# Powers of GpSimd later in its order, conv state stored in rows, the sample's indices copied earlier: a streaming encoder step on one core

## The chip, the core and the metric

The kernel runs on one core of a Trainium2 chip, as one program. The metric is the device time of one execution in microseconds. Three timed executions of the kernel before took 3982.19, 3983.57 and 3987.05 us; the median, 3983.57 us, is the time before.

## The reference, cut to what matters

One layer of a streaming encoder is computed for 1024 prompt rows and 32 sample rows. All arrays are fp32.

```
xn = rmsnorm(x);  z = xn @ w_in          # conv B | conv C | conv h | q | k | v | 2 gates
u  = C * h;  conv = B * dwconv3_causal(u)            # new state: last 2 rows of u
q, k = rope(rmsnorm(q)), rope(rmsnorm(k))            # 8 heads, two components each
o  = (softmax(Q1 K1^T) - lam * softmax(Q2 K2^T)) V;  o = rmsnorm(o) * (1 - lam0)
x  = x + (sig(gA) * (conv @ w_conv_out) + sig(gB) * (o @ w_attn_out)) @ w_o
# PEER, for each row and each of 8 heads:
q  = rmsnorm(xn2 @ wq);  s = q . subkeys             # 2 x 128 scores
best 16 of the 16 x 16 sums -> 16 experts e, weights g = softmax(best)
x  = x + sum_k g_k * gelu(u[e_k] . xn2) * v[e_k]     # 128 experts for each row
```

A row of 1024 values of `u` and one of `v` lie side by side in memory, 8 KB for each expert. The outputs are y, k and v of prompt and sample, and the two last rows of u of each (`conv_prompt` and `conv_sample`, 2 x 1024 each).

## The kernel before

**Rows and passes.** The rows are nine tiles: eight of 128 prompt rows (t = 0 to 7) and one of the 32 sample rows (t = 8). They go in three passes, rb = 0, 1 and 2, over tiles 0 to 2, 3 to 5, and 6 to 8. Each pass has two halves. `attend` goes through eight heads and three tiles: project, normalise and rotate q and k, scores, softmax, difference, weigh values, normalise the output. `middle` multiplies with the weight blocks `wall`: conv (24 blocks, in passes 1 and 2), gates and branch outputs (32), w_o (8), wq (16), and then searches the best keys (`find_tops`). Each block is 512 KB, loaded by SyncE into six buffers `low` (`load_mid`, L473), one when the block six places ahead of it has been used.

**The gather stream.** PEER has 1056 slots: 128 for each prompt tile, and 32 for the sample, whose 32 rows are spread four times over the 128 partitions. For slot q GpSimd gathers 128 rows of 8 KB, 1 MB, into buffer q % 8 of a ring (`gather`, L701), once slot q - 8 has been used. VectorE takes the dot product (`dot`, L1610), ScalarE makes gelu, weight and a diagonal (`slot`, L1224 to L1235), and TensorE adds weight times v (`weigh`, L991), in some slots VectorE (`add_row`, L1621). TensorE is one slot behind.

**What sets the order.** Every engine's program is written out from one list of positions. A position is a slot number; slots before 0 (from START = -340) have no gather. Each engine runs its generators up to position q and then does its part of slot q. GpSimd's own place is ahead of the others, since gather q waits only for slot q - 8: an instruction of GpSimd at position p + 8 comes about when the other engines are at p. GpSimd also makes the powers (x + eps)^-0.5: of q and k (`rr`, L672 and L674, after VectorE's `mean_square`, used by `scale_heads`), of the attention's output (`ro`, L663 and L666, after ScalarE's `square_out`, used by `norm_out`), of the row norm (`rx`) and of the PEER queries (`rq`, L689, four for each pass, after `find_tops` 3, 7, 11 and 15). POOL_LAG = 6 puts them 6 positions behind the step that makes their input; it stands in GpSimd's queue of gathers, and while a power waits for its input, no gather behind it is issued.

**Indices of the sample.** `routing` on VectorE chooses experts in 20 units; the last, of tile 8, ends at position 1017. The indices of tile 8 go into `idx[:, 0]`. At slot 1024 VectorE copies them and their weights into `idx[:, 1]` and `gw[:, 1]`, for each group of 32 partitions its own 32 slots (L1638, L1639), and raises `idx_ready`, on which gather 1024 waits.

**Conv state.** The last columns of u are kept as `ends_out`, channels in partitions. At m = 8 of the last pass SyncE stores them by four DMAs, one element in each run (L611), ahead of the weight loads that follow in its queue.

## Time and profile before

| | |
|---|---|
| median of three executions | 3983.57 us (3982.19 to 3987.05) |
| profiled execution, span from first to last instruction | 3979.7 us |
| its own time beside the span | not listed; the median is 3.9 us above the span |
| TensorE busy | 3171.9 us (80%) |
| VectorE busy | 2654.8 us (67%) |
| ScalarE, GpSimd busy | 1461.1 us (37%), 1531.1 us (38%) |
| moved by DMA | 1340.72 MB, of them 1108.54 MB by the gathers |
| mean granted TensorE clock | 0.872 |

The profile is of one execution. Busy shares are means over stages with different limits, so the stages have to be read one by one: the stretch up to about 600 us has no gathers; the attention of passes 1 and 2 lies at about 770 to 1250 us and 1800 to 2440 us; from about 3150 us on nearly only slots are left. DMA share is the busy share of the core's 16 DMA engines, GB/s what they moved in the stretch.

### The profile page before, as it was taken

What the parts mean: (1) busy time and instruction counts of PE and PEld (TensorE: products, weight loads), DVE (VectorE), ACT (ScalarE), POOL (GpSimd) and SP (SyncE); (2) the same over time, 40 slices, a digit from 0 to 9 for tenths busy, and PEclk for the clock granted to TensorE, in tenths of its full rate; (3) what the DMA queues carried; (4) which work ended last, traced back from release to release, by engine and by line L of the source; (5) the groups of instructions that cost most, each with busy time, mean ns of one, the idle gap of its engine ahead of it and who ended that gap; (6) DMA issues with size and microseconds to landing.
All of it is one profiled execution on the core that took longest, in us unless ns stands there. A gap on an engine that the chain in (4) does not pass through costs nothing.

```text
span 3979.7 us, 46667 instructions
## 1 busy us (share of the span) xinstructions
PE 3171.9 (80%) x14264; PEld 1436.6 (36%) x14264; DVE 2654.8 (67%) x6242; ACT 1461.1 (37%) x4359; POOL 1531.1 (38%) x1405
## 2 busy tenths in 40 slices
PE   6999988788987999797788887876879666666655
PEld 3555545333433554353333333544425211111110
DVE  3443016988888964778677876885568864556664
ACT  2222001355654244223456564233323333333332
POOL 2111002355655433434445554442344443444333
PEclk9999999889998999898899988888889776776676
DMA  4223336799999999988789999999999999999998
GB/s 157 97 92 102 101 122 257 266 354 340 408 365 387 416 417 392 403 342 342 293 333 375 377 352 397 416 362 368 400 420 404 370 420 420 420 420 419 411 394 346
DMA packets 257065, 1340.72 MB, mean 337 GB/s; under 512 B 31472, under 2 KB 70128, under 8 KB 121392
## 3 DMA queue, kind: packets, MB, share of 16 engines
q0 software_dynamic: 152400, 1108.54, 69.3%
q1 hardware_dynamic: 79344, 204.15, 14.0%
q10 hardware_dynamic: 25072, 25.04, 1.8%
q8 instruction: 115, 1.88, 0.2%
q14 instruction: 134, 1.10, 0.1%
HBM read 1310.49 MB, written 27.15 MB: 336 GB/s over the span
## 4 chain that ended last, share of the span: by engine, by line
PE 42%; DMA 24%; DVE 17%; ACT 6%; issue 4%; DVEq 3%; SPq 2%; ACTq 1%; POOL 1%; POOLq 0%
DMA ringx<-in_peer_uv,tl_idx 12%; DMA mix<-in_peer_uv,tl_idx 11%; PE tl_ps L939 9%; PE tl_ps L991 8%; PE tl_ps L775 6%; PE tl_ps L974 4%; PE tl_ps L923 3%; PE tl_ps L950 3%; PE tl_ps L840 3%; DVE ringx L1610 3%; DVE mix L1610 3%; PE tl_ps L753 2%; DVE tl_xa L1621 2%; PE tl_ps L809 2%; SPq L611 1%
## 5 line engine op out<-in xcount | busy, mean ns | idle before, releaser
L701 POOL DMA_INDIRECT mix<-in_peer_uv,tl_idx x528 | 626.0, 1186 | 782.9 <-PE tl_ps L991 432.8
L701 POOL DMA_INDIRECT ringx<-in_peer_uv,tl_idx x528 | 612.7, 1160 | 731.7 <-PE tl_ps L991 450.8
L1610 DVE CUSTOM_DVE_ANT_0 mix<-mix,tl_xb 128x1024 f32<-128x1024 f32 x528 | 640.9, 1222 | 296.2 <-DMA mix<-in_peer_uv,tl_idx 288.3
L1610 DVE CUSTOM_DVE_ANT_0 ringx<-ringx,tl_xb 128x1024 f32<-128x1024 f32 x528 | 640.7, 1222 | 277.8 <-DMA ringx<-in_peer_uv,tl_idx 270.1
L991 PE MATMUL tl_ps<-ringx,tl_dg 64*64 64x512 f32 x3352 | 569.7, 764 | 298.8 <-ACT tl_dg L1235 298.3
L991 PE MATMUL tl_ps<-mix,tl_dg 64*64 64x512 f32 x3288 | 566.9, 775 | 280.3 <-ACT tl_dg L1235 256.7
L1224 ACT ACTIVATE tl_hg<-tl_hd 128x1 f32<-128x1 f32 x1056 | 213.3, 202 | 1560.9 <-DVE tl_hd L1610 1545.8
L939 PE MATMUL tl_ps<-tl_xr,low 128*128 128x384 f32 (+1 forms) x1280 | 401.9, 470 | 32.2 <-DMA low<-in_wall 27.7
L1228 ACT ACTIVATE tl_hw<-tl_hg,tl_gw 128x1 f32<-128x1 f32 x1056 | 310.9, 294 | 76.1 <-issue 4.6
L991 PEld LDWEIGHTS tl_ps<-ringx,tl_dg 64*64 64x64 f32 x3352 | 105.6, 155 | 639.4 <-ACT tl_dg L1235 566.8
L991 PEld LDWEIGHTS tl_ps<-mix,tl_dg 64*64 64x64 f32 x3288 | 104.9, 157 | 617.8 <-ACT tl_dg L1235 512.6
L939 PEld LDWEIGHTS tl_ps<-tl_xr,low 128*128 128x128 f32 x1280 | 247.3, 197 | 201.0 <-issue 72.7
L1235 ACT ACTIVATE tl_dg<-tl_eye,tl_hw 128x64 f32<-128x64 f32 x830 | 288.6, 348 | 59.3 <-issue 1.7
L775 PE MATMUL tl_ps<-low,tl_xr 128*128 128x384 f32 (+1 forms) x768 | 298.5, 536 | 7.2 <-ACT tl_u L1101 7.0
L974 PE MATMUL tl_ps<-tl_xr,low 128*128 128x384 f32 (+1 forms) x768 | 262.6, 481 | 1.6 <-ACTq L1196 1.6
L923 PE MATMUL tl_ps<-tl_xr,low 128*128 128x384 f32 (+1 forms) x768 | 239.3, 471 | 0.6 <-ACT tl_xr L1080 0.6
L775 PEld LDWEIGHTS tl_ps<-low,tl_xr 128*128 128x128 f32 (+1 forms) x768 | 137.5, 189 | 185.0 <-issue 105.0
L974 PEld LDWEIGHTS tl_ps<-tl_xr,low 128*128 128x128 f32 x768 | 140.1, 195 | 135.2 <-issue 74.4
L923 PEld LDWEIGHTS tl_ps<-tl_xr,low 128*128 128x128 f32 x768 | 151.4, 201 | 102.5 <-issue 34.4
L672 POOL TENSOR_SCALAR tl_rr<-tl_ss 128x4 f32<-128x4 f32 (+1 forms) x72 | 61.5, 855 | 316.5 <-DVE tl_ss L1438 316.5
L1575 DVE TENSOR_TENSOR tl_u<-tl_ps,tl_u 128x384 f32<-128x384 f32 (+1 forms) x48 | 25.0, 521 | 197.5 <-PE tl_ps L939 195.3
L1621 DVE SCALAR_TENSOR_TENSOR tl_xa<-mix,tl_hw,tl_xa 128x1024 f32<-128x1024 f32 x117 | 149.8, 1281 | 3.7 <-issue 3.3
(193 smaller groups left out, 4002.1 us busy)
## 6 DMA issues: line engine op xcount, KB each, us to landing
low<-in_wall SPq DMA_DIRECT2D x240, 512.0 KB, 7.9
low<-in_watt SPq DMA_DIRECT2D x60, 512.0 KB, 9.0
mix<-in_peer_uv,tl_idx POOLq DMA_INDIRECT x528, 13.6
ringx<-in_peer_uv,tl_idx POOLq DMA_INDIRECT x528, 13.6
ringx<-in_watt SPq DMA_DIRECT2D x12, 512.0 KB, 5.9
tl_u<-in_x_prompt SPq DMA_DIRECT2D x8, 512.0 KB, 11.8
x_rows<-tl_u SPq DMA_DIRECT2D x8, 512.0 KB, 8.1
xs_rows<-tl_u SPq DMA_DIRECT2D x8, 512.0 KB, 7.5
```

The lines of the kernel that those rows point to most:

```text
L701: nc.gpsimd.indirect_dma_start(out=ring[q % RING].rearrange("p a d -> p (a d)"), out_offset=None, in_=A["peer_uv"], in_offset=bass.Indirec ...
L775: last = nc.tensor.matmul(o, xn[:, c, i * P:i * P + n], w[:, :, c, :], start=(c == 0), stop=(c == DC - 1))
L840: last = nc.tensor.matmul(ps[:, (3, 5, 3)[k], 0:nr], w[:, c, :], xn[:, c, 0:nr], start=(c == 0), stop=(c == DC - 1))
L923: last = nc.tensor.matmul(ps[:, 2 + 3 * (cc % 2) + k, 0:n], w[:, c, :], xnr[:, c, 0:n], start=(c == 0), stop=(c == DC - 1))
L939: last = nc.tensor.matmul(ps[:, 2 + k, 0:n], w[:, c, :], src[k][:, c, 0:n], start=(c == 0), stop=(c == DC - 1))
L974: last = nc.tensor.matmul(ps[:, 2 + qb % 2, 0:n], w[:, c, :], xT[:, c, 0:n], start=(c == 0), stop=(c == DC - 1))
L991: last = nc.tensor.matmul(ps[half_of(h), b, :], dg[rows, npe(q) % DIAGS, :], ring[q % RING][rows, 1, h * 512:(h + 1) * 512], start=k == 0, ...
L1224: nc.scalar.activation(hg[:, j:j + 1], hd[:, j:j + 1], ACT.Gelu)
L1228: gate = nc.scalar.activation(hw[:, j:j + 1], hg[:, j:j + 1], ACT.Copy, scale=gw[:, table(t), k:k + 1])
L1235: nc.scalar.activation(dg[:, npe(q) % DIAGS, :], eye[:], ACT.Copy, scale=hw[:, j:j + 1]).then_inc(s["dg_done"], 1)
L1610: nc.vector.tensor_tensor_reduce(out=ring[q % RING][:, 0, :], in0=ring[q % RING][:, 0, :], in1=xb[:, t % 2, :], scale=1.0, scalar=0.0, op0 ...
L1621: nc.vector.scalar_tensor_tensor(out=xa[:], in0=ring[q % RING][:, 1, :], scalar=hw[:, k % TOPK:k % TOPK + 1], in1=xa[:], op0=ALU.mult, op1 ...
```

## The change

Three things are changed.

1. In passes 1 and 2 the powers of q and k stand 8.5 positions behind their input instead of 6, those of the attention output 9 instead of 6, and those of the PEER queries 13 instead of 9, in all passes but for the first of them. VectorE's uses move too, in passes 1 and 2: `scale_heads` from 1.0 to 2.6 units, and `norm_out` from 4.2 to 5.6 units, behind `rotate` and `mean_square` (a unit is 0.75 slots in pass 1, 0.93 in pass 2).
2. The conv state is transposed by TensorE into bank 6 (32 rows of 128), copied by ScalarE into `Y`, and stored by four DMAs of 8 rows of 512 bytes at m = 20 of the last pass.
3. The copies for the sample come right behind the last unit of `routing`, and go into `itop` and `tops`, which the sample's gathers and weights read.

```diff
+RR_LAG, RO_LAG, RQ_LAG = 8.5, 9, 13
-RO, KP, SH = 2.2, 2.2, 1.0
+RO, KP, SH, SH_LATE = 2.2, 2.2, 1.0, 2.6
-        def table(t):
+        def table(own, spread, t):
-            return t % 2 if t < NT else 1
+            return own[:, t % 2] if t < NT else spread[:, 0, 0:DEC // TOPK].rearrange("p a b -> p (a b)")
 # SyncE
-                    if m == 8 and rb + 1 == PASSES:
-                        sp.wait_ge(s["y_done"], 3 * DC)
+                    if m == 20 and rb + 1 == PASSES:
+                        sp.wait_ge(s["st_c"], 1)
...
-                                    sp.dma_start(A[name][j].rearrange("(c p) -> p c", p=P),
-                                                 ends_out[:, 2 * k + j, :]).then_inc(s["cvo_out"], 16)
+                                sp.dma_start(A[name][j].rearrange("(c p) -> c p", p=P),
+                                             Y[(2 * k + j) * DC:(2 * k + j + 1) * DC, 0:P]).then_inc(s["cvo_out"], 16)
 # GpSimd
-                        yield step_at(rb, h, base + PV + 0.6) + (POOL_LAG if rb else 0)
+                        yield step_at(rb, h, base + PV + 0.6) + (RO_LAG if rb else 0)
-                        yield step_at(rb, h, base + PJ + 2.6) + (POOL_LAG if rb else 0)
+                        yield step_at(rb, h, base + PJ + 2.6) + (RR_LAG if rb else 0)
-                    yield ends[43 + 4 * quad] + (3 + POOL_LAG if rb or quad else 3)
+                    yield ends[43 + 4 * quad] + (RQ_LAG if rb or quad else 3)
-                    in_offset=bass.IndirectOffsetOnAxis(ap=idx[:, table(t), k:k + 1], axis=0)).then_inc(landed[q % RING], 16)
+                    in_offset=bass.IndirectOffsetOnAxis(ap=table(idx, itop, t)[:, k:k + 1], axis=0)).then_inc(landed[q % RING], 16)
 # TensorE, block 6 of the gates, and ahead of the first block of w_o
+                            if j == 6 and rb + 1 == PASSES:
+                                pe.wait_ge(s["y_done"], PASSES * DC)
+                                nc.tensor.transpose(ps[:4 * DC, 6, 0:P], ends_out[:].rearrange("p a c -> p (a c)"), ident[:]).then_inc(s["st_t"], 1)
+                                if rb + 1 == PASSES:
+                                    pe.wait_ge(s["st_c"], 1)
 # ScalarE, behind the gate of block 8
+                        if cc == 2 and k == 0 and rb + 1 == PASSES:
+                            act.wait_ge(s["st_t"], 1)
+                            nc.scalar.copy(Y[:4 * DC, 0:P], ps[:4 * DC, 6, 0:P]).then_inc(s["st_c"], 1)
 # VectorE, end of routing(); the same copies at slot 1024 are removed
+                for quad in [slice(p * DEC, (p + 1) * DEC) for p in range(P // DEC)]:
+                    nc.vector.tensor_copy(table(idx, itop, NT)[quad], idx[quad, 0, quad])
+                    nc.vector.tensor_copy(table(gw, tops, NT)[quad], gw[quad, 0, quad])
+                nc.vector.drain().then_inc(s["idx_ready"], 1)
+                dve.sem_inc(s["gw_done"], 1)
 # VectorE, attend
-                        yield step_at(rb, h, base + SH)
+                        yield step_at(rb, h, base + (SH_LATE if rb else SH))
-                    if u > 0:
+                    if u > 0 and rb == 0:
                         yield step_at(rb, h, base + TO - 0.8)
                         norm_out(DC * rb + before[0], before[1])
...
+                    if u > 0 and rb:
+                        yield step_at(rb, h, base + TO + 0.6)
+                        norm_out(DC * rb + before[0], before[1])
```

SyncE's queue in the last pass, before (`low` are weight blocks, `ends_out` is the conv state with channels in partitions):

```order
L569 DMA tl_u1<-in_x_sample 32x1024
L611 DMA out_conv_prompt<-tl_ends_out 128x8x1
L611 DMA out_conv_sample<-tl_ends_out 128x8x1
L611 DMA out_conv_prompt<-tl_ends_out 128x8x1
L611 DMA out_conv_sample<-tl_ends_out 128x8x1
L473 DMA low<-in_wall 128x1024 x36
```

The same place after the change:

```order
L570 DMA tl_u1<-in_x_sample 32x1024
L474 DMA low<-in_wall 128x1024 x12
L611 DMA out_conv_prompt<-tl_Y 8x128
L611 DMA out_conv_sample<-tl_Y 8x128
L611 DMA out_conv_prompt<-tl_Y 8x128
L611 DMA out_conv_sample<-tl_Y 8x128
L474 DMA low<-in_wall 128x1024 x24
```

Twelve weight loads now stand ahead of the four stores, which have become 8 rows of 128 values.

GpSimd's queue in the attention of pass 1, before (`mix` and `ringx` are the two halves of the ring; both pieces start with the same gather, number 99):

```order
L701 DMA mix<-in_peer_uv,tl_idx 128x2048
L701 DMA ringx<-in_peer_uv,tl_idx 128x2048
L663 TENSOR_SCALAR tl_ro<-tl_so 128x1
L666 TENSOR_TENSOR tl_ro<-tl_ro,mhalf 128x1
L701 DMA ringx<-in_peer_uv,tl_idx 128x2048 x3
L672 TENSOR_SCALAR tl_rr<-tl_ss 128x4
L674 TENSOR_TENSOR tl_rr<-tl_rr,mhalf 128x4
L701 DMA mix<-in_peer_uv,tl_idx 128x2048 x3
```

The same place after the change:

```order
L701 DMA mix<-in_peer_uv,tl_idx 128x2048
L701 DMA ringx<-in_peer_uv,tl_idx 128x2048
L672 TENSOR_SCALAR tl_rr<-tl_ss 128x4
L674 TENSOR_TENSOR tl_rr<-tl_rr,mhalf 128x4
L701 DMA ringx<-in_peer_uv,tl_idx 128x2048 x3
L663 TENSOR_SCALAR tl_ro<-tl_so 128x1
L666 TENSOR_TENSOR tl_ro<-tl_ro,mhalf 128x1
L701 DMA mix<-in_peer_uv,tl_idx 128x2048 x3
```

The `rr` that now stands behind gather 100 stood two gathers earlier, and the `ro` that stood there has three gathers more ahead of it. Counted through the pass, each `rr` has 2 or 3 gathers more ahead of it, each `ro` 3, each `rq` 4 (the last `rq` has 732 instead of 728); VectorE's `scale_heads` has one or two more dot products ahead of it, `norm_out` one.

VectorE's queue from slot 1017 on, before (`tl_best` are the weights of the last unit):

```order
L1367 TENSOR_REDUCE tl_gs<-tl_best 128x4
L1369 RECIPROCAL tl_gs<-tl_gs 128x4
L1371 TENSOR_TENSOR tl_gw<-tl_best,tl_gs 128x64
L1610 ISA mix,tl_hd<-mix,tl_xb 128x1024
L1610 ISA tl_hd 128x1
...
L1638 COPY tl_idx<-tl_idx 32x32
L1639 COPY tl_gw<-tl_gw 32x32
```

The same place after the change:

```order
L1375 TENSOR_REDUCE tl_gs<-tl_best 128x4
L1377 RECIPROCAL tl_gs<-tl_gs 128x4
L1379 TENSOR_TENSOR tl_gw<-tl_best,tl_gs 128x64
L1403 COPY tl_itop<-tl_idx 32x32
L1404 COPY tl_tops<-tl_gw 32x32
```

The eight copies stood behind six dot products more (slots 1018 to 1023).

## Rows read from the trace of the kernel before

**Rows 1.** The profile page: busy us of each engine, share of the span, instructions.
```profile
PE 3171.9 (80%) x14264; PEld 1436.6 (36%) x14264; DVE 2654.8 (67%) x6242; ACT 1461.1 (37%) x4359; POOL 1531.1 (38%) x1405
```
**Rows 2.** Busy time by stretch; attention of passes 1 and 2, and slots alone.
```profile
core 0: us, PE busy (x) PEld busy (x) DVE busy (x) ACT busy (x) POOL busy (x), PEclk, DMA share, GB/s
...
770.00:1250.00 480.00, 381.02 (x2057) 173.46 (x2055) 411.82 (x975) 271.60 (x776) 265.57 (x244) 0.91 0.93 362
...
1800.00:2440.00 640.00, 508.90 (x2626) 209.62 (x2626) 494.43 (x1100) 337.01 (x908) 319.30 (x278) 0.87 0.91 352
...
3150.00:3500.00 350.00, 227.25 (x1120) 41.02 (x1112) 207.38 (x381) 120.18 (x418) 145.34 (x139) 0.69 1.01 420
```
**Rows 3.** Timeline of SyncE's queue, 2600 to 2800 us: start, duration, line.
```profile
2638.11 34.17 SPq L611 DMA_DIRECT2D out_conv_prompt<-tl_ends_out  x1
2672.32 22.32 SPq L611 DMA_DIRECT2D out_conv_sample<-tl_ends_out  x1
2694.69 103.81 SPq L473 DMA_DIRECT2D low<-in_wall  x21
```
**Rows 4.** Timeline of TensorE, 2640 to 2725 us, idle time before it in brackets.
```profile
2707.01 3.22 PE L939 MATMUL tl_ps<-tl_xr,low 128*128 128x288 f32 x6 [27.68 <-DMA low<-in_wall]
```
**Rows 5.** Busy time by stretch around these stores.
```profile
2640.00:2660.00 20.00, 12.67 (x57) 7.84 (x55) 14.26 (x22) 6.02 (x14) 5.83 (x5) 0.90 1.08 341
2660.00:2680.00 20.00, 15.24 (x52) 9.52 (x48) 17.63 (x26) 7.24 (x19) 7.83 (x6) 0.76 1.10 303
2680.00:2712.00 32.00, 4.99 (x17) 2.75 (x18) 8.39 (x11) 5.40 (x12) 1.24 (x2) 0.57 0.76 238
```
**Rows 6.** Timeline of VectorE: dot products of slots 1012, 1023, 1024 and 1055.
```profile
3852.10 1.22 DVE L1610 CUSTOM_DVE_ANT_0 ringx<-ringx,tl_xb 128x1024 f32<-128x1024 f32 x1 [1.27 <-DMA ringx<-in_peer_uv,tl_idx]
...
3879.80 1.23 DVE L1610 CUSTOM_DVE_ANT_0 ringx<-ringx,tl_xb 128x1024 f32<-128x1024 f32 x1 [1.54 <-DMA ringx<-in_peer_uv,tl_idx]
...
3887.87 1.23 DVE L1610 CUSTOM_DVE_ANT_0 mix<-mix,tl_xb 128x1024 f32<-128x1024 f32 x1 [5.85 <-DMA mix<-in_peer_uv,tl_idx]
...
3969.17 1.22 DVE L1610 CUSTOM_DVE_ANT_0 ringx<-ringx,tl_xb 128x1024 f32<-128x1024 f32 x1 [1.24 <-DMA ringx<-in_peer_uv,tl_idx]
```
**Rows 7.** Timeline of GpSimd: gather 1024.
```profile
3882.32 0.94 POOL L701 DMA_INDIRECT mix<-in_peer_uv,tl_idx  x1 [15.72 <-DVEq L1640]
```
**Rows 8.** Busy time by stretch: around gather 1024.
```profile
3870.00:3890.00 20.00, 9.02 (x56) 1.63 (x48) 7.89 (x20) 4.95 (x18) 6.07 (x6) 0.78 0.54 204
```
**Rows 9.** Timeline of GpSimd: the last power of PEER queries.
```profile
3118.86 1.46 POOL L689 TENSOR_TENSOR tl_rq<-tl_qse,mhalf 128x6 f32<-128x6 f32 x1 [11.45 <-DVE tl_qse L1302]
```
**Rows 10.** Busy time by stretch: around that power.
```profile
3110.00:3122.00 12.00, 7.50 (x36) 3.83 (x36) 11.19 (x53) 1.69 (x6) 2.65 (x3) 0.64 0.26 107
```
**Rows 11.** Timeline of VectorE between gathers' stop and that power: two dot products.
```profile
3112.19 1.20 DVE L1610 CUSTOM_DVE_ANT_0 mix<-mix,tl_xb 128x1024 f32<-128x1024 f32 x1
3113.32 1.22 DVE L1610 CUSTOM_DVE_ANT_0 mix<-mix,tl_xb 128x1024 f32<-128x1024 f32 x1
```
**Rows 12.** Waits of GpSimd, 770 to 1250 us: total, times, longest.
```profile
POOL tl_rr L672 <- DVE tl_ss L1438: 94.4, 24, 11.0
```
**Rows 13.** Waits of GpSimd, 1800 to 2440 us.
```profile
POOL tl_rr L672 <- DVE tl_ss L1438: 81.5, 23, 7.9
...
POOL tl_ro L663 <- ACT tl_u L1073: 52.8, 18, 6.4
```
**Rows 14.** Waits of VectorE for gathers, 1590 to 1800 us.
```profile
DVE ringx L1610 <- DMA ringx<-in_peer_uv,tl_idx: 8.5, 6, 1.9
DVE mix L1610 <- DMA mix<-in_peer_uv,tl_idx: 6.8, 5, 1.9
```
**Rows 15.** Waits of VectorE for gathers, 1800 to 2440 us.
```profile
DVE ringx L1610 <- DMA ringx<-in_peer_uv,tl_idx: 9.3, 5, 2.5
...
DVE mix L1610 <- DMA mix<-in_peer_uv,tl_idx: 5.1, 4, 2.4
```
**Rows 16.** Timeline of one power in pass 1, on GpSimd, and its use on VectorE.
```profile
909.16 1.08 POOL L674 TENSOR_TENSOR tl_rr<-tl_rr,mhalf 128x4 f32<-128x4 f32 x1
...
917.38 0.49 DVE L1468 TENSOR_TENSOR tl_u<-tl_u,tl_rr 128x128 f32<-128x128 f32 x2 [0.16 <-issue]
```

More of the change, by code:

```diff
@@ L605, in _ @@
                         sp.dma_start(rope[:, 0:3], A["rope"][:, 3 * (rb + 1):3 * (rb + 1) + 3]).then_inc(s["rope_in"], 16)
-                    if m == 8 and rb + 1 == PASSES:
-                        sp.wait_ge(s["y_done"], 3 * DC)
-                        with nc.allow_non_contiguous_dma(reason="two rows of state, channels in partitions"):
-                            for j in range(2):
-                                for k, name in enumerate(("conv_prompt", "conv_sample")):
-                                    sp.dma_start(A[name][j].rearrange("(c p) -> p c", p=P),
-                                                 ends_out[:, 2 * k + j, :]).then_inc(s["cvo_out"], 16)
+                    if m == 20 and rb + 1 == PASSES:
+                        sp.wait_ge(s["st_c"], 1)
+                        for j in range(2):
+                            for k, name in enumerate(("conv_prompt", "conv_sample")):
+                                sp.dma_start(A[name][j].rearrange("(c p) -> c p", p=P),
+                                             Y[(2 * k + j) * DC:(2 * k + j + 1) * DC, 0:P]).then_inc(s["cvo_out"], 16)
             sp.wait_ge(s["acc_done"], NT + 2)
```

12 lines of the change are left out of this document (2 added, 10 removed).

## Prediction, made before the changed kernel was run

> **What bounds the kernel now.** The page's busy shares come first [rows 1]: no engine is above 80%, so none explains the time by itself, and the stages have to be read apart. The table by stretch does that [rows 2]. Where nearly only slots are left, from 3150 us on, the DMA engines are busy all the time (1.01) and move 420 GB/s; one gather of 1.05 MB takes 1.05 MB / 420 GB/s = 2.5 us, and the dot products stand at that distance: from slot 1012 to slot 1023 there are 27.70 us for 11 slots, 2.52 us each [rows 6]. So the last part is bound by bytes, and every microsecond in which the DMA engines stood still earlier comes back as time. In the attention of passes 1 and 2 DMA is at 0.93 and 0.91 and moves 362 and 352 GB/s [rows 2]; VectorE is busy for 411.82 of 480 us in pass 1 (86%) and 494.43 of 640 us in pass 2 (77%), TensorE for 79% and 80%. There no resource is full, and what is late is decided by waits between engines. I therefore count a change by lost DMA time where DMA is otherwise full, and by waits on VectorE in the two attentions.
>
> The sum is made against the profiled execution, span 3979.7 us; the median of the timed runs is 3983.57 us, 3.9 us more, and that difference is carried over unchanged.
>
> **Conv state.** The stores take SyncE's queue from 2638.11 to 2694.69 us [rows 3]: 2 x 2048 elements in 4096 runs of 4 bytes in 56.6 us, 13.8 ns each. Behind them the next weight block waits, and TensorE stands for 27.68 us until it lands [rows 4]. TensorE's wait is not the price, since gathers in flight go on meanwhile and slots catch up afterwards. The price in DMA: from 2640 to 2712 us were moved 20 x 341 + 20 x 303 + 32 x 238 = 20496 units [rows 5], which at 420 GB/s need 48.8 us; 72 - 48.8 = 23.2 us are lost. In the first 40 us the engines are "busy" at 1.08 to 1.10 and move only 303 to 341 GB/s: the small runs take their time. In the last 32 us they stand idle at 0.76. The price cannot be above TensorE's wait plus the first part's loss, 27.7 + (40 - 40 x 322 / 420 = 9.3) = 37 us, nor below 13.9 us, the last 32 us alone (32 - 32 x 238 / 420). I take 23.
>
> The Trainium skill, "DMA: Bandwidth & Descriptors", section Specifications, gives a limit of about 358 GB/s for the HBM side of one core. By it the same 72 us would have lost only 72 - 20496 / 358 = 14.7 us, and the attentions, at 362 and 352 GB/s, would be full already. The trace disagrees: 420 GB/s over 350 us [rows 2].
>
> What is added in place of the stores: one TensorE transpose, one ScalarE copy of 32 x 128, and four stores of 4 KB in 32 runs. ScalarE is at 37% and TensorE waits in this half anyway; I bound the two from above by one gather issue each, 0.94 us [rows 7], and take 0.5 us together. The stores stand behind 12 more weight loads, and the copy that they wait for is made at block 8, while the load ahead of them (m = 20) waits for block 14: SyncE does not stop there, and nothing behind it is late. TensorE's new wait ahead of w_o is for a copy made more than 20 blocks earlier. Four stores at SyncE: nothing above 2 us, below the distance of the loads around them (103.81 us for 21, 4.9 us each [rows 3]); hidden, and if not, 2 us. The same page of the Trainium skill, section Bandwidth, measures 0.68 us for 4 KB and calls transfers under 64 KB "descriptor-dominated"; four would be 2.7 us of DMA spans, and the sum would be 20.3 instead of 22.5 us for this part if they were not spread. No row here shows such a store.
>
> **The sample's indices.** GpSimd stands for 15.72 us until VectorE has made the copies at slot 1024 [rows 7]. The ring runs empty: 20 us at 204 GB/s lose 20 - 20 x 204 / 420 = 10.3 us [rows 8]. From the dot products: slot 1023 to 1055 are 89.37 us for 32 slots; at 2.5 us they would be 80.0, so 9.4 us are lost; the gap from 1023 to 1024 alone is 8.07 us, 5.6 over the usual distance [rows 6]. After the change `idx_ready` comes behind slot 1017, when gather 1024 becomes free through slot 1016: at most one slot late, with seven gathers in flight. The eight copies take about 1.1 us of VectorE, whose dot product is 1.23 us of 2.5. I take 9, with ends 5.6 and 10.3.
>
> **The powers of the PEER queries.** The last one stops GpSimd for 11.45 us [rows 9], and in 3110 to 3122 us DMA moves 107 GB/s: 12 - 12 x 107 / 420 = 8.9 us lost, in a stretch beside which DMA is full [rows 10]. Now four more gathers stand ahead of it. Not all can be issued, since each needs a slot freed, and VectorE is busy for 11.19 of these 12 us: while GpSimd stands, two slots are done (3112.19, 3113.32 [rows 11]), and one just before. Two or three gathers of 2.5 us: 5 to 7.5 us; I take 6, with ends 0 (VectorE's search is then the bound) and 8.9. The nine others with gathers around them move likewise; what they give lies in the waits of the next part.
>
> **The powers in the attention.** GpSimd waits 94.4 us for `rr` in pass 1 [rows 12], 81.5 us for `rr` and 52.8 us for `ro` in pass 2 [rows 13]. Two or three gathers more ahead of each power, and these waits all but vanish. But this is not the gain, since eight gathers are in flight and a late issue mostly costs nothing: VectorE waits for gathers only 8.5 + 6.8 = 15.3 us in the last part of pass 1 [rows 14] and 9.3 + 5.1 = 14.4 us in pass 2's attention [rows 15]. Together 29.7 us; part of it is DMA being full, part would be followed by the next wait. I take 8. The ends: upward, DMA full through both attentions: (1 - 362/420) x 480 + (1 - 352/420) x 640 = 66 + 104 = 170 us, of which stalls of ordering will leave at least three quarters, so 45; downward, a loss by late uses. For these the order gives room: a power of `rr` is behind the gather that needs slot 29 freed where its input comes at VectorE's 31st dot product, and its use moves from the 33rd to the 34th. In the trace the power ended at 910.24 and was used at 917.38 us, 7.1 us later [rows 16]; two gathers and a wait vanish or come ahead, one slot of about 3.3 us (480 us for 145 slots) is added to the room. I see no wait of VectorE in the mean, and take none; its price is in the rivals.
>
> The sum: 23 - 0.5 + 9 + 6 + 8 = 45.5 us off the span of 3979.7, so a span near 3934, and a time of 3983.6 - 45.5 = **3938 us**.
>
> **Rivals.**
> A: the powers give nothing. Conv state and sample alone are 31.5 us: 3952 us. For it: GpSimd's waits are hidden by seven buffers, as VectorE's 14.4 us of waits in 640 show. Against it: 107 GB/s in rows 10 is a hole with GpSimd's stop right at it. With a small loss by the powers it reaches 3970.
> B: the attentions speed up more. GpSimd stands there for 94 to 134 us a pass, DMA has 170 us of room, VectorE 68 + 146 us. If a quarter of that room is used: 31.5 + 6 + 43 = 80 us, 3903 us. Against it: VectorE, at 86% in pass 1, has waits on ScalarE and TensorE that this doesn't touch.
> C, slower: the powers become late. Each of 96 uses (24 of `rr` and 24 of `ro` in each attention) then waits on VectorE for a gather issue and a power, 0.94 + 1.08 = 2.0 us [rows 7, 16], 194 us; VectorE's idle time takes about half: 97 - 37.5 (conv, sample, PEER powers) = 59.5 us more than before, 4043 us. It decides from 37.5 / 96 = 0.4 us uncovered a use. Against it: room of one or two slots for each.
> D: the stores were not what held TensorE, and the block would be late anyway, by full DMA: then 9 + 6 + 8 - 0.5 = 22.5 us, 3961 us. Against it: SyncE issues the block only at 2694.69, right behind them.
>
> **How the numbers follow.** Forecast 0.52, A 0.20, B 0.14, D 0.06, C 0.04, and 0.04 for a smaller loss by late powers that eats the gain and ends near the time before. The forecast's own range is 3922 to 3950. The range for 8 in 10 is 3906 to 3964: down nearly to B, up beyond A and D. A change of 0.2%, 8 us, is what a measurement of this kernel can tell from none. Faster by more: 0.52 + 0.20 + 0.14 + 0.06 = 0.92, less 0.01 for A's loss: 0.91; within: 0.05; slower: 0.04.
>
> **What would show it.** Conv: no idle time of SyncE's length near 2640 us, TensorE never 27 us idle for `low`, 400 GB/s or more through the stretch. Sample: the gap between dot products 1023 and 1024 near 2.5 us, no wait of GpSimd on it. PEER powers: the stretch before the tail with no 12 us at 107 GB/s, and L689's waits below 3 us. Attention: L672's and L663's waits near zero, and the two attentions shorter by about 8 us in all. Wrong: these waits gone and the attentions as long as before (A), much shorter (B), or VectorE waiting for L674 or L666 by tens of us (C).

## The result, and the profile after

The changed kernel takes 3949.99 us in the median of four executions (3944.02 to 3952.07), beside 3983.02 us (3982.19 to 3987.05, four executions) for the kernel before. The ratio is 0.9913, with a 95% interval of 0.9899 to 0.9927: 0.87% faster, 34.7 us by the ratio and 33.0 us by the two medians. That is inside the range of 3906 to 3964 us, 12 us above the 3938 us that were predicted, and 2 us from the 3952 us of rival A. The profiled execution has a span of 3942.2 us and a time of 3944.02, the fastest of the four.

The page, busy time of each engine and what the DMA engines carried [rows 1]:

```profile
PE 3151.6 (80%) x14265; PEld 1430.7 (36%) x14265; DVE 2656.8 (67%) x6242; ACT 1461.2 (37%) x4360; POOL 1487.7 (38%) x1405
...
DMA packets 252970, 1340.72 MB, mean 340 GB/s; under 512 B 27345, under 2 KB 66033, under 8 KB 117297
```

The bytes are the same. The page of the kernel before has 257065 packets, 31472 of them under 512 B: 4127 small ones are gone, the 4096 elements of the conv state and a few more, and the 32 rows of 512 bytes have come. No engine has less to compute; GpSimd runs the same 1405 instructions in 43.4 us less.

A table that one makes oneself shows where the time went: the start of VectorE's dot product of each slot, read from both timelines, and the time between two such starts. A slot does nearly the same work in both, so a difference belongs to the stretch in which it arises.

```
us from slot to slot   0-25  25-175  175-300  300-343  343-544  544-580  580-608  608-712  712-768  768-1023  1023-1055
before                110.0   493.3    417.6    173.3    685.8    111.2    115.0    323.5    148.2     651.4       89.4
after                 110.0   495.0    418.1    174.0    675.6    111.5     91.6    323.8    147.6     651.0       82.7
```

Slots 25 to 175 are the attention of pass 1, 343 to 544 that of pass 2, 580 to 608 the stretch of the conv stores, 712 to 768 the search of the last pass, and 1023 to 1055 the sample. Three stretches gain: 10.2, 23.4 and 6.7 us. One loses a little, 1.7 us, and the search stays where it was.

**Conv state.** SyncE's queue, timeline from 2632 us, start and duration first [rows 3]:

```profile
2632.43 73.98 SPq L474 DMA_DIRECT2D low<-in_wall  x12
2706.45 0.38 SPq L611 DMA_DIRECT2D out_conv_prompt<-tl_Y  x1
2706.87 0.30 SPq L611 DMA_DIRECT2D out_conv_sample<-tl_Y  x1
```

Two of the four stores are shown; the others take 0.29 and 0.30 us. 56.6 us of a blocked queue (57.5 with the first two of the four old stores, which took 0.42 and 0.58 us) have become 1.3. In the same stretch TensorE has no wait for `low` left. Busy time by stretch, columns as in [rows 2] [rows 5]:

```profile
2640.00:2660.00 20.00, 12.12 (x46) 7.46 (x44) 16.80 (x21) 5.90 (x14) 8.05 (x6) 0.83 1.02 402
2660.00:2680.00 20.00, 14.88 (x70) 9.29 (x70) 14.94 (x23) 10.79 (x24) 9.61 (x7) 0.97 1.01 417
2680.00:2712.00 32.00, 28.39 (x117) 18.71 (x114) 23.89 (x39) 13.69 (x31) 12.81 (x11) 0.91 1.01 417
```

Where 341, 303 and 238 GB/s stood, there are now 402, 417 and 417.

**Sample.** GpSimd's gather 1024, and VectorE's dot products of slots 1023 and 1024 [rows 6, 7]:

```profile
3836.36 0.94 POOL L701 DMA_INDIRECT mix<-in_peer_uv,tl_itop  x1 [1.37 <-DVEq L1405]
```
```profile
3848.03 1.23 DVE L1626 CUSTOM_DVE_ANT_0 ringx<-ringx,tl_xb 128x1024 f32<-128x1024 f32 x1 [1.38 <-DMA ringx<-in_peer_uv,tl_idx]
...
3850.63 1.22 DVE L1626 CUSTOM_DVE_ANT_0 mix<-mix,tl_xb 128x1024 f32<-128x1024 f32 x1 [1.37 <-DMA mix<-in_peer_uv,tl_itop]
```

GpSimd's wait fell from 15.72 to 1.37 us, and the gap between the two dot products from 8.07 to 2.60. Over the place of the old hole the DMA engines stay nearly full, where there had been 204 GB/s [rows 8]:

```profile
3840.00:3850.00 10.00, 8.04 (x36) 1.22 (x32) 4.94 (x8) 3.28 (x13) 3.74 (x4) 0.52 1.01 419
3850.00:3860.00 10.00, 6.59 (x40) 1.50 (x40) 4.93 (x8) 4.30 (x14) 4.08 (x4) 0.83 1.01 420
```

**The last power of the PEER queries.** GpSimd's timeline around it [rows 9], and busy time by stretch [rows 10]:

```profile
3084.40 0.95 POOL L701 DMA_INDIRECT mix<-in_peer_uv,tl_idx  x1 [7.80 <-PE tl_ps L996]
...
3095.55 1.76 POOL L701 DMA_INDIRECT mix<-in_peer_uv,tl_idx  x1 [7.58 <-PE tl_ps L996]
3097.34 1.67 POOL L689 TENSOR_TENSOR tl_rq<-tl_qse,mhalf 128x6 f32<-128x6 f32 x1
```
```profile
3076.00:3088.00 12.00, 7.06 (x36) 3.73 (x36) 11.46 (x58) 3.40 (x13) 3.44 (x4) 0.72 0.64 225
3088.00:3100.00 12.00, 5.40 (x24) 1.24 (x24) 11.19 (x24) 2.54 (x9) 4.24 (x3) 0.57 0.68 262
```

The power no longer waits (11.45 us before), and the hole of 107 GB/s is gone. But the gathers around it now wait 7.80 and 7.58 us themselves, for a buffer that TensorE has yet to use (L996 is `weigh`), and there are two stretches at 225 and 262 GB/s. The third of the busy times, VectorE's, suggests why: it is busy for 11.46 and 11.19 of 12 us. A hole was filled, and nobody seems to have waited for what fills it; e4_rq_back, f3_units_last and g2_rq_units below test this.

**The attention.** GpSimd's waits for the inputs of the powers are gone: of 94.4 us for `rr` in pass 1 [rows 12] 4.9 are left, of 81.5 and 52.8 in pass 2 [rows 13] none that the view lists. Its gathers wait in their place; in pass 2 (1800 to 2440 us) for TensorE, with 100.9 and 92.0 us:

```profile
POOL ringx L701 <- PE tl_ps L996: 100.9, 35, 11.0
POOL mix L701 <- PE tl_ps L996: 92.0, 43, 9.4
```

What this did to VectorE's waits can be read over the same slots in both kernels. Slots 343 to 544, before (VectorE's waits for gathers and powers: total, times, longest):

```profile
DVE mix L1610 <- DMA mix<-in_peer_uv,tl_idx: 14.6, 9, 3.0
DVE ringx L1610 <- DMA ringx<-in_peer_uv,tl_idx: 14.3, 8, 2.5
DVE tl_u L1484 <- POOL tl_ro L666: 0.8, 1, 0.8
```

and after:

```profile
DVE tl_u L1497 <- POOL tl_ro L666: 6.6, 2, 3.5
DVE mix L1626 <- DMA mix<-in_peer_uv,tl_idx: 5.6, 4, 2.0
DVE ringx L1626 <- DMA ringx<-in_peer_uv,tl_idx: 3.8, 4, 1.3
DVE tl_u L1481 <- POOL tl_rr L674: 1.2, 1, 1.2
```

28.9 us of waits for gathers became 9.4, and 0.8 us for powers became 7.8. In pass 1 (slots 25 to 175) the same exchange goes the other way round: there were only 5.2 us of waits for gathers to win, 0.5 are left, and 0.9 us of waits for powers became 12.1, namely

```profile
DVE tl_u L1497 <- POOL tl_ro L666: 8.0, 9, 2.6
DVE tl_u L1481 <- POOL tl_rr L674: 4.1, 3, 2.3
```

These waits are not where pass 2 became shorter. All 28.9 us of them stood in slots 400 to 544, and so do the 9.4 that are left; these slots take 475.0 us instead of 475.7, and VectorE's waits for ScalarE there have grown from 28.0 to 39.5 us. The gain is in slots 343 to 400, 200.5 instead of 210.1 us, where VectorE had waited for no gather at all, and 8.5 us of it lie in slots 370 to 385. Busy time by stretch of just these 15 slots, before and after:

```profile
1934.70:1993.97 59.27, 52.54 (x257) 21.73 (x261) 37.59 (x81) 28.21 (x79) 30.41 (x26) 0.79 0.81 296
```
```profile
1936.75:1987.56 50.81, 45.02 (x257) 18.84 (x253) 37.14 (x79) 28.26 (x78) 26.92 (x26) 0.92 0.97 357
```

TensorE is busy for 89% of the stretch both times. It does the same 257 matmuls in 7.5 us less, at a granted clock (the column behind the busy times) of 0.92 instead of 0.79. Once more in finer steps, 12 us from the end of a pause of TensorE, before and after:

```profile
1933.10:1945.10 12.00, 11.53 (x40) 5.20 (x41) 8.77 (x18) 2.48 (x8) 7.97 (x6) 0.50 0.70 269
```
```profile
1935.20:1947.20 12.00, 9.24 (x53) 4.11 (x53) 8.93 (x20) 5.68 (x17) 8.17 (x7) 0.88 0.75 269
```

In both kernels TensorE had nearly nothing to do in the 3 us ahead of it (0.00 and 0.03 us busy), and came back at the lower of its two levels, 0.50 of full speed. Before, it stayed there for these 12 us; in the changed kernel for 3 us (0.52), then it ran at 1.00.

### The profile page after: what moved, and what is told of

It reads as the page before. It is cut to its first block, busy times and chain, and to the rows that moved or that the text cites. A ratio compares the mean times of both kernels' runs of the same rounds, so it can differ in the third digit from the quotient of the medians.

```text
span 3942.2 us, 46670 instructions
## 1 busy us (share of the span) xinstructions
PE 3151.6 (80%) x14265; PEld 1430.7 (36%) x14265; DVE 2656.8 (67%) x6242; ACT 1461.2 (37%) x4360; POOL 1487.7 (38%) x1405
## 3 DMA queue, kind: packets, MB, share of 16 engines
q1 hardware_dynamic: 75248, 204.15, 13.9%
## 4 chain that ended last, share of the span: by engine, by line
PE 42%; DMA 23%; DVE 17%; ACT 7%; issue 5%; DVEq 3%; POOL 1%; ACTq 1%; SPq 0%; POOLq 0%
DMA mix<-in_peer_uv,tl_idx 11%; DMA ringx<-in_peer_uv,tl_idx 9%; PE tl_ps L942 8%; PE tl_ps L996 8%; PE tl_ps L775 6%; PE tl_ps L979 4%; PE tl_ps L923 4%; PE tl_ps L955 3%; PE tl_ps L840 3%; DVE ringx L1626 3%; DVE mix L1626 3%; DVE tl_xa L1637 2%; PE tl_ps L753 2%; DMA ringx<-in_peer_uv,tl_itop 2%; PE tl_ps L809 2%
## 5 line engine op out<-in xcount | busy, mean ns | idle before, releaser
L996 PE MATMUL tl_ps<-ringx,tl_dg 64*64 64x512 f32 x3352 | 567.1, 761 | 293.6 <-ACT tl_dg L1243 292.9
L996 PE MATMUL tl_ps<-mix,tl_dg 64*64 64x512 f32 x3288 | 561.4, 769 | 282.8 <-ACT tl_dg L1243 263.4
L1232 ACT ACTIVATE tl_hg<-tl_hd 128x1 f32<-128x1 f32 x1056 | 213.3, 202 | 1508.6 <-DVE tl_hd L1626 1482.9
L996 PEld LDWEIGHTS tl_ps<-ringx,tl_dg 64*64 64x64 f32 x3352 | 105.6, 154 | 633.2 <-ACT tl_dg L1243 557.9
L1236 ACT ACTIVATE tl_hw<-tl_hg,tl_gw 128x1 f32<-128x1 f32 x1024 | 301.5, 294 | 74.4 <-issue 5.1
L996 PEld LDWEIGHTS tl_ps<-mix,tl_dg 64*64 64x64 f32 x3288 | 105.3, 156 | 615.8 <-ACT tl_dg L1243 510.3
L775 PEld LDWEIGHTS tl_ps<-low,tl_xr 128*128 128x128 f32 (+1 forms) x768 | 138.1, 190 | 190.9 <-issue 108.1
L1637 DVE SCALAR_TENSOR_TENSOR tl_xa<-ringx,tl_hw,tl_xa 128x1024 f32<-128x1024 f32 x109 | 139.6, 1281 | 3.8 <-issue 3.6
```

The source lines that it names most:

```text
L775: last = nc.tensor.matmul(o, xn[:, c, i * P:i * P + n], w[:, :, c, :], start=(c == 0), stop=(c == DC - 1))
L996: last = nc.tensor.matmul(ps[half_of(h), b, :], dg[rows, npe(q) % DIAGS, :], ring[q % RING][rows, 1, h * 512:(h + 1) * 512], start=k == 0, ...
L1232: nc.scalar.activation(hg[:, j:j + 1], hd[:, j:j + 1], ACT.Gelu)
L1236: gate = nc.scalar.activation(hw[:, j:j + 1], hg[:, j:j + 1], ACT.Copy, scale=table(gw, tops, t)[:, k:k + 1])
L1637: nc.vector.scalar_tensor_tensor(out=xa[:], in0=ring[q % RING][:, 1, :], scalar=hw[:, k % TOPK:k % TOPK + 1], in1=xa[:], op0=ALU.mult, op1 ...
```

## Experiments

The runs e1 to e4, f1 to f4 and g0 to g4 are three groups; beside each group the kernel before ran on the same chip, 3981.1 to 3985.1 us in the median. A ratio is that of a kernel to the kernel before, with its 95% interval. "before +" and "after +" say from which of the two an edit starts.

### One part at a time

**e1_conv**: before + the conv state's part of the change alone (transpose, copy, stores of rows at m = 20).

```diff
-                    if m == 8 and rb + 1 == PASSES:
-                        sp.wait_ge(s["y_done"], 3 * DC)
+                    if m == 20 and rb + 1 == PASSES:
+                        sp.wait_ge(s["st_c"], 1)
...
+                                nc.tensor.transpose(ps[:4 * DC, 6, 0:P], ends_out[:].rearrange("p a c -> p (a c)"), ident[:]).then_inc(s["st_t"], 1)
...
+                            nc.scalar.copy(Y[:4 * DC, 0:P], ps[:4 * DC, 6, 0:P]).then_inc(s["st_c"], 1)
```

> The kernel before with the conv state's part alone (transpose, copy, four stores of 512-byte rows at m = 20). Theory (the stores took 23 us of DMA time, and nothing else held TensorE): 23 us faster than before, give or take 3. Rival (the block would have been late anyway): under 5 us. Rival (TensorE's whole wait comes back): 28 us or more.

Measured: 3966.64 us, 0.9952 [0.9935, 0.9969], 19 us less, with 12 to 26 in the interval. Slots 580 to 608 take 92.6 us instead of 115.0, as in the changed kernel; the others are unmoved but for the attention of pass 2, where this execution lost 8.5 us (694.3 instead of 685.8) with an order of instructions that is the old one there. So the stores cost about 22 us of their own stretch in this execution, and an execution scatters by as much as some terms of the sum. Rows instead of elements and m = 20 instead of m = 8 were changed together; neither was run alone at the old place.

**e2_sample**: before + the sample's copies alone.

```diff
-                if q == NT * SLOTS:
-                    for p in range(4):
...
+                for quad in [slice(p * DEC, (p + 1) * DEC) for p in range(P // DEC)]:
+                    nc.vector.tensor_copy(table(idx, itop, NT)[quad], idx[quad, 0, quad])
```

> The kernel before with the sample's copies alone behind the last unit of routing. By the times of the dot products of the two traces (the distance to the kernel before grows from 31.8 us at slot 1023 to 38.4 us at slot 1055) 6 to 7 us faster than before; by the prediction's count of lost DMA time 9. Rival (waits of the ring's tail take it back): 0 to 2 us.

Measured: 3977.63 us, 0.9982 [0.9972, 0.9993]: 7 us less. Slots 1023 to 1055 take 82.8 us instead of 89.4.

**e3_powers**: before + the three lags and VectorE's later uses alone.

```diff
+RR_LAG, RO_LAG, RQ_LAG = 8.5, 9, 13
-RO, KP, SH = 2.2, 2.2, 1.0
+RO, KP, SH, SH_LATE = 2.2, 2.2, 1.0, 2.6
```

> The kernel before with the lags of GpSimd's powers and VectorE's later uses alone. Theory now (the attention of pass 2 gets the 8 us by which the traces differ at slot 544, pass 1 and the PEER powers nothing): 4 to 8 us faster. Rival A (hidden by the ring, the 8 us are scatter between executions): within 2 us of before. Rival C (late uses): slower by 3 us or more.

Measured: 3978.26 us, 0.9983 [0.9973, 0.9994]: 7 us less. Pass 2's attention takes 678.5 us instead of 685.8, pass 1's 497.0 instead of 493.3, the search 147.8 instead of 148.2. The stores still stand in this kernel, and cost less than before: 106.7 us for slots 580 to 608, 15 above the 91.6 without them. SyncE's queue, timeline from 2636 us, and TensorE's wait behind it:

```profile
2636.02 33.18 SPq L612 DMA_DIRECT2D out_conv_prompt<-tl_ends_out  x1
2669.24 14.36 SPq L612 DMA_DIRECT2D out_conv_sample<-tl_ends_out  x1
```
```profile
PE tl_ps L940 <- DMA low<-in_wall: 25.1, 1, 25.1
```

The queue stood 9 us less long here, TensorE 2.6 us less. The same four stores cost 15 to 23 us. In this kernel's own gain of 11 us of span, these cheaper stores are 8 us, and whether they come from the later powers or from chance isn't settled by one execution (e2_sample, with the old powers, has 114.2 us there).

The three parts alone are 19 + 7 + 7 = 33 us, each with an interval of 4 to 7 us to either side; together they gave 34.7 us, and 29.6 in the repetition f1_after_again. Within these intervals they add.

**e4_rq_back**: after + the lag of the PEER queries' powers as before.

```diff
-RR_LAG, RO_LAG, RQ_LAG = 8.5, 9, 13
+RR_LAG, RO_LAG, RQ_LAG = 8.5, 9, 9
```

> The changed kernel with RQ_LAG back at 9 of 13, the rest as it is. The prediction's term would make it 6 us slower than the changed kernel. Theory now (in the search of the last pass VectorE is busy for more than 90% and is itself the bound, so an earlier gather finds no earlier use): within 2 us of the changed kernel, with the wait of about 11 us of L689 back.

**f1_after_again** is the changed kernel once more, unchanged, beside f2_runs_last, f3_units_last and f4_units_both.

> The changed kernel once more, beside the three below on one chip: 33 to 35 us faster than before, as measured first. If the parts add up (19 us conv state, 7 us sample, 7 us powers, each alone against before) it comes out at 33.

Measured: 3952.76 us, 0.9918 [0.9903, 0.9933]; f1_after_again took 3952.3 us, 0.9927 [0.9914, 0.9941], 29.6 us less than before and not the expected 33 to 35. These intervals are 11 to 12 us wide, so the times alone wouldn't show the predicted 6 us; the stretch does. L689's last wait is back (9.94 us), and with it the hole:

```profile
3090.00:3102.00 12.00, 6.20 (x35) 3.13 (x34) 11.25 (x49) 1.69 (x6) 3.24 (x3) 0.78 0.28 100
```

Yet slots 712 to 768 take 147.9 us here, and 147.6 and 148.7 in the two executions of the changed kernel. Slots 712 to 725, in which the hole lies, take the same 43.85 us in e4_rq_back and after, VectorE busy for 41.27 of them in both:

```profile
3059.60:3103.45 43.85, 31.41 (x182) 16.23 (x180) 41.27 (x166) 12.74 (x48) 18.65 (x15) 0.86 0.76 304
```
```profile
3049.39:3093.24 43.85, 31.57 (x185) 16.71 (x183) 41.27 (x164) 12.74 (x48) 14.17 (x14) 0.87 0.87 339
```

What the DMA engines moved less in them is made up in slots 725 to 745 (415 GB/s, 370 in after). This part of the change gives nothing.

### What the runs of 4 bytes cost

**f2_runs_last**: after + the old stores of single elements in place of the rows, issued by SyncE behind its last load, so that they block nothing.

```diff
-                    if m == 20 and rb + 1 == PASSES:
-                        sp.wait_ge(s["st_c"], 1)
...
+            sp.wait_ge(s["y_done"], 3 * DC)
+                        sp.dma_start(A[name][j].rearrange("(c p) -> p c", p=P), ends_out[:, 2 * k + j, :]).then_inc(s["cvo_out"], 16)
```

> The changed kernel, but with the conv state stored as before in runs of 4 bytes, issued by SyncE behind its last load, where no load waits behind them. Theory (the price was two things: about 9 us of DMA time in the first 40 us, in which small runs displaced gathers, and about 14 us in which the ring stood still behind TensorE's wait for the block): 6 to 12 us slower than the changed kernel. Rival (only the blocked queue cost anything): within 2 us of it. Rival (all of it was DMA time): 18 us or more slower.

Measured: 3951.03 us, 0.9927 [0.9913, 0.9941]: the same as the changed kernel, as the first rival had it and not the theory. The two long ones of the four stores fell at 3027 to 3069 us, and took their time from the DMA engines there (busy time by stretch):

```profile
3040.00:3060.00 20.00, 20.00 (x117) 11.75 (x118) 17.48 (x76) 6.53 (x26) 7.81 (x7) 1.00 1.01 364
3060.00:3080.00 20.00, 17.19 (x106) 8.44 (x104) 18.78 (x76) 6.24 (x24) 8.15 (x9) 1.00 1.01 356
```

364 and 356 GB/s instead of about 420: some 6 us of transfers are pushed back. The last part of the search begins there (slot 712 at 3052.68 us), where VectorE is the bound and the DMA engines have time left over. They catch up: slots 712 to 768 take 148.4 us. A run that was to price the bytes priced a place where they are free, so it was repeated in another.

**g1_runs_tail**: f3_units_last (below) + the same stores of single elements in place of the rows, issued only once tile 6 is done (slot 896), where only slots are left and DMA is full.

```diff
+            sp.wait_ge(s["y_done"], 3 * DC)
+            sp.wait_ge(s["acc_done"], NT - 1)
+                        sp.dma_start(A[name][j].rearrange("(c p) -> p c", p=P), ends_out[:, 2 * k + j, :]).then_inc(s["cvo_out"], 16)
```

> The same, but the conv state stored in runs of 4 bytes by SyncE when tile 6 is finished (slot 896 on), where DMA is full, no load waits behind the stores, and no hole follows in which lost DMA time could be made up. Theory (the runs displace gathers; behind the last load they cost nothing only because the hole of the last search stood behind them): 5 to 10 us slower than the one with units moved, and GB/s near 300 to 370 for some 40 us. Rival (small runs cost the gathers nothing, only the blocked queue did): within 2 us.

Measured: 3957.62 us, 0.9930 [0.9911, 0.9949], beside 3942.39 us without them: 15 us by the medians. Slots 900 to 1012 take 301.7 us instead of 288.5: 13.2 us. SyncE's queue, and the stretch of the stores:

```profile
3529.18 24.06 SPq L612 DMA_DIRECT2D out_conv_prompt<-tl_ends_out  x1
3553.29 22.03 SPq L612 DMA_DIRECT2D out_conv_sample<-tl_ends_out  x1
```
```profile
3540.00:3560.00 20.00, 11.16 (x52) 1.93 (x56) 10.24 (x23) 5.91 (x21) 7.78 (x7) 0.59 1.02 352
3560.00:3580.00 20.00, 13.30 (x56) 1.94 (x53) 13.78 (x32) 5.67 (x21) 8.10 (x6) 0.50 1.01 361
3580.00:3600.00 20.00, 10.71 (x56) 2.25 (x56) 13.15 (x22) 5.31 (x19) 7.15 (x7) 0.62 1.01 324
3600.00:3620.00 20.00, 9.71 (x56) 1.77 (x48) 10.74 (x17) 5.47 (x20) 7.36 (x7) 0.72 1.01 359
```

Here nothing waits behind the stores, and 4096 runs of 4 bytes, 16 KB, still cost as much as the gathers of five slots, at a DMA share of 1.01 and 324 to 361 GB/s. In these 80 us were moved 20 x (352 + 361 + 324 + 359) = 27920 units, which need 66.5 us at 420 GB/s: 13.5 us are lost, and the dot products lost 13.2. If the runs cost the same at their old place, which was not measured there, some 13 of the 23 us are the DMA engines' time for the runs, and the rest, about 10, is the queue that they block: gathers that are not asked for while TensorE stands without its weight block. The first 40 us at the old place alone would say 9 and 14.

### Why the search did not move

The theory after e4: where the hole lies VectorE is the bound, and an earlier gather is worth nothing. Then less work for VectorE in the search must help.

**f3_units_last**: after + the two turns at which VectorE chooses the experts of tile 6 (`routing`, two units of four heads each) moved later, out of the search. Each pair of numbers is one unit: the slot of its first piece, and how many slots lie between two of its pieces. A unit has nine pieces, so (713, 3) goes from slot 713 to 737.

```diff
-           (388, 4), (450, 5), (514, 5), (560, 5), (713, 3), (745, 4), (850, 4), (900, 4), (950, 4), (985, 4))
+           (388, 4), (450, 5), (514, 5), (560, 5), (725, 3), (752, 4), (850, 4), (900, 4), (950, 4), (985, 4))
```

> The changed kernel with VectorE's choices for tile 6 moved from slots 713 to 777 to slots 725 to 784, out of the key search of the last pass, where VectorE is busy for 95% and DMA moves 225 and 262 GB/s for 24 us. Theory (VectorE is the bound of that hole, not GpSimd's powers): three or four choices of about 3 us leave it, 5 to 9 us faster than the changed kernel. Rival (the hole is set by GpSimd or by gathers in flight): within 2 us.

**g0_units_again** is the same kernel once more, beside g1_runs_tail, g2_rq_units and g4_tile3_spread.

> The kernel with tile 6's choices moved to slots 725 to 784, once more, as the measure for the three beside it: 1.0% faster than before, 40 to 45 us.

Measured: 3939.67 us, 0.9898 [0.9883, 0.9913], and again 3942.39 us, 0.9894 [0.9875, 0.9914]: 10 to 13 us less than the changed kernel, and the fastest version of all. The forecast was 5 to 9. Slots 712 to 768 take 138.7 and 138.1 us instead of 147.6, and nearly all of that is in slots 712 to 725, 35.3 us in both executions. Busy time over just these slots, g0_units_again (the changed kernel's row stands at e4_rq_back):

```profile
3047.11:3082.44 35.33, 28.93 (x185) 15.10 (x183) 30.88 (x130) 12.75 (x48) 17.49 (x14) 0.98 0.99 391
```

VectorE has 10.4 us less to do in them (30.88 instead of 41.27), and the 13 slots are 8.5 us shorter. The kernel before, after, e4, f1 and f2 all have the old units there, differ in the lag of `rq` and in the GB/s (304 to 339), and take 43.82 to 43.86 us. So the bound of this place is VectorE. Behind it VectorE gets the work back, 42.0 us of it in slots 725 to 745 instead of 33.2, and that costs nothing: 44.4 and 45.1 us instead of 45.6. It had time there (33.2 of 45.6 us busy after), and has more further on (slots 768 to 1023 take 651.9 us, 651.0 after). What has changed with it is that the DMA engines are now full from slot 712 on (a share of 0.99 to 1.01, where after had 0.87, 0.92 and 1.01 in slots 712 to 725, 745 and 768).

**g2_rq_units**: f3_units_last + RQ_LAG 9, to see whether the lag of the powers counts once VectorE isn't the bound of slots 712 to 725.

```diff
-RR_LAG, RO_LAG, RQ_LAG = 8.5, 9, 13
+RR_LAG, RO_LAG, RQ_LAG = 8.5, 9, 9
```

> The same as the one with units moved, with RQ_LAG back at 9. Theory (the PEER powers' lag was worth nothing only because VectorE had the hole to itself; with its choices gone, GpSimd's stop of some 10 us is next): 3 to 7 us slower than the one with units moved. Rival (the lag never matters): within 2 us.

Measured: 3949.11 us, 0.9917 [0.9900, 0.9935]; slots 712 to 768 take 143.4 us. Timeline of GpSimd and busy time of the same 12 us, first with lag 13 (g0_units_again):

```profile
3085.71 1.35 POOL L689 TENSOR_TENSOR tl_rq<-tl_qse,mhalf 128x6 f32<-128x6 f32 x1
...
3084.00:3096.00 12.00, 7.65 (x48) 1.66 (x44) 11.19 (x29) 4.36 (x16) 9.03 (x7) 0.78 0.97 369
```

and with lag 9 (g2_rq_units):

```profile
3084.49 2.26 POOL L689 TENSOR_TENSOR tl_rq<-tl_qse,mhalf 128x6 f32<-128x6 f32 x1 [7.36 <-DVE tl_qse L1310]
...
3084.00:3096.00 12.00, 7.38 (x40) 1.77 (x44) 11.29 (x31) 5.07 (x18) 9.49 (x8) 0.77 0.67 257
```

VectorE is as busy in one as in the other (11.19 and 11.29 us). The wait of 7.36 us leaves a stretch at 257 GB/s, and now it isn't made up, since the DMA engines have no time left behind it. VectorE runs dry after the hole, not in it. Slots 725 to 745, lag 13 and then lag 9:

```profile
3082.44:3126.88 44.44, 29.86 (x164) 7.40 (x168) 41.95 (x91) 16.90 (x61) 22.33 (x19) 0.73 1.00 407
```
```profile
3086.61:3137.87 51.26, 33.62 (x168) 7.17 (x172) 42.52 (x91) 17.75 (x63) 26.93 (x24) 0.67 0.96 392
```

6.8 us are lost there, 5 in slots 712 to 768 and 6.7 by the medians (the two intervals overlap, so the total alone would not show it). With VectorE relieved, this part of the change is worth the 5 to 6 us that were predicted for it without that.

**f4_units_both** and **g4_tile3_spread**: f3_units_last + the same for tile 3 in the search of pass 1, once farther, once less far.

```diff
-UNIT_AT = (... (170, 5), (321, 3), (346, 3),
+UNIT_AT = (... (170, 5), (338, 3), (364, 3),      # f4_units_both
+UNIT_AT = (... (170, 5), (324, 4), (358, 3),      # g4_tile3_spread
```

> As the one with tile 6's choices moved, and tile 3's moved too, from slots 321 to 370 to slots 338 to 388, out of the search of pass 1 into the attention of pass 2. Theory: the search of pass 1 (DMA at 167 to 300 GB/s for 65 us) gains 5 us or so, but the attention, with VectorE at 77%, gives part back: 0 to 5 us faster than with tile 6 alone. Rival (the attention is bound by waits round VectorE): slower than with tile 6 alone by 3 us or more.

> The same as the one with units moved, with tile 3's choices at slots 324, 328, 332, 336 and 358 to 382 in place of 321 to 370. Half of them leave the search of pass 1, half of the work comes into the attention's first slots. By the trace with all moved (4 us gained in the search, 14 us lost in the attention from slot 343 to 400): 1 to 6 us slower than the one with units moved. Rival (only the bunching with the first heads of the attention cost anything): 1 to 4 us faster.

Measured: 3950.71 us, 0.9918 [0.9903, 0.9932], and 3949.16 us, 0.9912 [0.9893, 0.9930]. The search of pass 1 (slots 300 to 343) gains: 168.5 and 170.0 us instead of 174.5 and 173.8. The attention behind it loses more: 689.5 and 688.3 us for slots 343 to 544, where f3_units_last and g0_units_again have 672.7 and 671.9, and the nine executions with the later powers and the old place of tile 3's choices 671.9 to 680.4. By the medians they are 11.0 and 6.8 us slower than f3_units_last beside each, with intervals that overlap; forecast were 0 to 5 us faster for the first and 1 to 6 slower for the second. The loss is all in slots 343 to 400 (214.8 and 213.3 us instead of 200.1 to 205.8). In f4_units_both VectorE is busy 13.9 us longer there (167.6 instead of 153.7 us), in g4_tile3_spread only 4.2. In both, slots 370 to 385 take 59 us, at a granted clock of 0.84 and 0.78, as they did in the kernel before. So the choices landed in VectorE's way in the first, and for the second the cause was not settled.

## Why the prediction was right, and where it was not

**Conv state: 23 predicted, 23.4 measured.** The count of lost DMA time over 72 us, taken at 420 GB/s, gave the size to within 1 us. By the 358 GB/s of the Trainium skill, "DMA: Bandwidth & Descriptors", section Specifications, it would have been 14.7, and a core at 417 GB/s in this very stretch shows that the figure isn't this core's bound. What the count could not say is how much is the runs' own time and how much the blocked queue: 9.3 us by the rate of the first 40 us, and g1_runs_tail has 13 in another place. Rival D is refuted: with the old stores gone, no wait for `low` is left. That the count hit to 1 us is in part luck: the same stores cost 15 us in e3_powers. The replacements were put at 0.5 us, and none of them can be found in the stretch. The 2.7 us that the prediction worked out for the four stores from the 0.68 us of the Trainium skill, "DMA: Bandwidth & Descriptors", section Bandwidth (a figure for loads from HBM issued by GpSimd), can't be found either: they take 1.3 us of SyncE's queue, and nothing waits for them. The same page of the Trainium skill, section Rules for kernel authors, says that a strided last dimension is lowered to one descriptor per element; the 4127 packets fewer under 512 B agree.

**Sample: 9 predicted, 6.7 measured.** Right in kind, a quarter too large. The term took the last 32 slots down to 2.5 us each, the pace of the stretch before them; they go at 82.7 / 32 = 2.58. The better base was the gap between two dot products, 8.07 - 2.5 = 5.6, which was one of the ends.

**Powers of the PEER queries: 6 predicted, nothing measured. This is the step that failed.** It read: VectorE is busy for 11.19 of these 12 us, but while GpSimd stands two slots are done, so two or three gathers more can be issued, 5 to 7.5 us. They were issued (the hole of 107 GB/s is gone) and they were not needed: in slots 712 to 725 VectorE had 41.3 us of its own work in 43.85, with dot products of gathers already landed, and the DMA engines had time left behind it to make up what a hole had cost (e4_rq_back). The prediction's own rule was that lost DMA time counts where DMA is otherwise full, and it took this place for one. f3_units_last takes VectorE's work away and wins 9.5 us; then DMA is full, and g2_rq_units shows the 5 us of the lag. The 0 was one of the ends of this term, and the row that decided for it, 11.19 of 12, stood beside the one that was believed.

**Powers in the attention: 8 predicted, 7 to 9 measured, and the agreement is luck.** With the old order in this place (before, e1_conv, e2_sample) pass 2's attention takes 685.8, 694.3 and 687.8 us, mean 689.3; with the new order (after, f1, e4, f2, e3) 675.6, 679.2, 680.4, 677.7 and 678.5, mean 678.3: 11 us less. The four others with the new order there, f3, g0, g1 and g2, have 671.9 to 679.3. Pass 1's takes 493.3, 493.4 and 496.6, mean 494.4, and in the same five kernels 495.0 to 497.4, mean 496.7: 2 more. So the order makes a difference, but not by the step that the term was built on, VectorE's waits for gathers. Half of its base, the 15.3 us at 1590 to 1800 us, lies behind the attention of pass 1, in slots 175 to 343, and is 16.7 us after the change; those slots gained nothing (417.6 and 173.3 us, 418.1 and 174.0 after). The attention of pass 1 had only 5.2 us. In pass 2 the waits did fall, by 19.5 us, and the slots in which they stood stayed as long as they were.

What became shorter is slots 370 to 385: 59.27 us in all three executions with the old order, 50.8 to 51.0 in seven with the new one and 54.0 in two (e3_powers, g1_runs_tail). There TensorE is busy for 89%, and in the kernel before it works 12 us at the lower level of its clock where the changed kernel has 3. That the clock sets the length of the stretch follows from this share; no run changed the clock alone. No term of the prediction has this; it is the second step that failed, behind a number that came out. Why the clock comes back sooner in the new order no run shows, and it isn't known which of the moves (`rr`, `ro`, `scale_heads`, `norm_out`) is needed for it: they were not run apart, nor was the new order in pass 2 alone.

The waits of GpSimd, 228.7 us before (94.4 + 81.5 + 52.8), said nothing of the gain, and those of VectorE for gathers said nothing either. The room for the later powers was not as large as the prediction's one example had it: they come late 12 times in pass 1, by 1 us in the mean. That is the mechanism of rival C, and it is real at a tenth of the size that C gave it (11.2 + 7.0 = 18.2 us more of waits instead of 194). Rival A said that the ring hides GpSimd's waits. For the gathers of the changed kernel that is what the runs show, and its 3952 us are nearer to the 3949.99 and 3952.3 us of the changed kernel than the forecast is.

The sum of what was measured is 23.4 + 6.7 + 0 + 8 = 38 us by the profile's stretches (the two spans differ by 37.5) and 33.0 to 34.7 by the timed runs (29.6 in the repetition), against 45.5 predicted. The 7.5 us between 45.5 and 38 are the PEER powers (6) and the sample (2). The remaining 3 to 5 us are no more than what executions scatter: the profiled one was the fastest of its four.
